# Feed-forward and conformer of a decoder step in passes over one token chunk, with vector operands kept in PSUM

## What is computed

```python
def swiglu(x, wg, wu, wd):
    return (jax.nn.silu(x @ wg) * (x @ wu)) @ wd

def conformer_conv(xn, buf, w_pw1, b_pw1, w_dw, b_dw, ln_g, ln_b, w_pw2, b_pw2):
    a, gate = jnp.split(xn @ w_pw1 + b_pw1, 2, axis=-1)
    h = a * jax.nn.sigmoid(gate)
    x_ext = jnp.concatenate([buf.astype(h.dtype), h], axis=1)
    buf_new = x_ext[:, -(CONV_W - 1):]
    h = causal_dwconv(x_ext, w_dw) + b_dw
    h = jax.nn.silu(layer_norm(h, ln_g, ln_b))
    return h @ w_pw2 + b_pw2, buf_new

# layer 0: x += mixer(rms_norm(x));      x += swiglu(rms_norm(x))
# layer 1: x += conformer(rms_norm(x));  x += swiglu(rms_norm(x));  y = rms_norm(x)
```

## Time and profile before

| | |
|---|---|
| median of 3 runs | 2816.01 us (2814.19 to 2819.28) |
| the profiled execution | 2820.21 us, of which the span 2818.4 us |
| PE, DVE, ACT, POOL busy | 98%, 50%, 31%, 24% of the span |
| chain that ended last | PE 62%, POOL 7%, DVE 2% |
| granted TensorE clock | 0.996 of full speed |

### The profile page before, as it was taken

How to read it: one execution, slowest core, us unless ns; L and a number is a source line. 1 busy time by engine, 2 the same in 40 slices (tenths; PEclk the granted TensorE clock), 3 DMA queues, 4 the chain that set the end, 5 groups by cost and what they waited for, 6 DMA issues and landing times.

```text
span 2818.4 us, 41854 instructions
## 1 busy us (share of the span) xinstructions
PE 2759.0 (98%) x15649; PEld 2419.5 (86%) x15649; DVE 1421.2 (50%) x2692; ACT 859.8 (31%) x1500; POOL 675.5 (24%) x333
## 2 busy tenths in 40 slices
PE   7999999999999999999999999999999999999998
PEld 5886666689866999999999986665699999999998
DVE  4227768889966532232232258997353222322325
ACT  2227739844423211111111034555221111111113
POOL 0210025511001322222222108991022222222220
PEclk9999999999999999999999999999999999999999
DMA  4220067634572211111111111110121111111101
GB/s 152 87 91 8 16 193 222 183 95 140 174 258 75 68 53 45 45 45 45 45 45 45 38 35 40 38 38 3 45 83 45 45 45 52 51 45 45 45 23 61
DMA packets 211508, 204.42 MB, mean 73 GB/s; under 512 B 10477, under 2 KB 165714, under 8 KB 211116
## 3 DMA queue, kind: packets, MB, share of 16 engines
q1 hardware_dynamic: 200014, 186.27, 21.7%
q0 software_dynamic: 2992, 12.26, 1.4%
q10 hardware_dynamic: 8390, 4.40, 0.6%
HBM read 187.59 MB, written 17.14 MB: 73 GB/s over the span
## 4 chain that ended last, share of the span: by engine, by line
PE 62%; POOL 7%; DVE 2%; DMA 1%; ACT 1%; issue 1%; SPq 0%; POOLq 0%; DVEq 0%; ACTq 0%
PE bank L2717 17%; PE bank L2718 17%; PE bank L2719 17%; POOL big L2994 6%; PE bank L364 3%; PE bank L2399 3%; PE bank L3047 1%; DMA res_b<-park 1%; PE bank L316 1%; POOL big L3000 1%; DVE tmp L303 1%; DVE res_b L2864 0%; DVE big L330 0%; DVE res_a L330 0%; ACT tmp L289 0%
## 5 line engine op out<-in xcount | busy, mean ns | idle before, releaser
L2717 PE MATMUL bank<-xh,wh 128*128 128x344 f32 x2112 | 675.3, 320 | 0.0
L2719 PE MATMUL bank<-xh,wl 128*128 128x344 f32 x2112 | 673.9, 319 | 0.0
L2718 PE MATMUL bank<-xl,wh 128*128 128x344 f32 x2112 | 673.5, 319 | 0.0
L2838 POOL TENSOR_TENSOR wl<-wring,wh 128x1024 fp32r<-128x1024 f32 x128 | 318.0, 2508 | 1111.1 <-ACT wh L2768 1111.0
L2856 DVE TENSOR_TENSOR tmp<-bank,tmp 128x344 f32<-128x344 f32 x132 | 68.1, 516 | 779.5 <-PE bank L2719 773.4
L2717 PEld LDWEIGHTS bank<-xh,wh 128*128 128x128 f32 x2112 | 397.4, 188 | 0.4
L2719 PEld LDWEIGHTS bank<-xh,wl 128*128 128x128 f32 x2112 | 396.7, 188 | 0.0
L2718 PEld LDWEIGHTS bank<-xl,wh 128*128 128x128 f32 x2112 | 396.0, 188 | 0.4
L2864 DVE TENSOR_TENSOR res_b<-res_b,bank 128x344 f32<-128x344 f32 x528 | 268.3, 512 | 199.7 <-PE bank L2719 199.5
L2717 PE MATMUL bank<-hh,wh 128*128 128x344 f32 x1056 | 339.2, 321 | 0.0
L2718 PE MATMUL bank<-hl,wh 128*128 128x344 f32 x1056 | 337.9, 320 | 0.0
(11 more groups left out here) (436 smaller groups left out, 3712.6 us busy)
## 6 DMA issues: line engine op xcount, KB each, us to landing
big<-in_cache_attn_k SPq DMA_DIRECT2D x128, 256.0 KB, 3.0
big<-in_cache_attn_v SPq DMA_DIRECT2D x128, 256.0 KB, 2.9
wring<-in_ffn_w_down SPq DMA_DIRECT2D x44, 512.0 KB, 3.3
wring<-in_ffn_w_gate SPq DMA_DIRECT2D x42, 512.0 KB, 3.8
wring<-in_ffn_w_up SPq DMA_DIRECT2D x42, 512.0 KB, 3.9
wring<-in_conv_w_pw SPq DMA_DIRECT2D x24, 512.0 KB, 4.0
wring<-in_w_in SPq DMA_DIRECT2D x20, 512.0 KB, 4.0
park<-res_a SPq DMA_DIRECT2D x1, 4128.0 KB, 11.2
```

The lines of the kernel that those rows point to most:

```text
L2717: pe.matmul(bank_out, h, mh, start=(n == 0), stop=False)
L2718: pe.matmul(bank_out, h, ml, start=False, stop=False)
L2719: mm = pe.matmul(bank_out, l, mh, start=False, stop=(n == len(terms) - 1))
L2838: pool.tensor_tensor(wl[u][:, :], raw, wh[u][:, :].bitcast(F32), ALU.subtract).then_inc(w_cut, 1)
```

## The change

The two feed-forwards and the conformer become one sequence (`late_pe`, `late_act`, `late_dve`, `late_pool`, `late_sp`) of six passes; pass p does all 11 rounds of a layer for one chunk. Passes 0 to 2 are layer 0 on chunks 0 to 2, passes 3 to 5 layer 1.

- Between the passes stand the pointwise products of the conformer for one chunk: pw1 of chunk 0 behind pass 1; pw2 of chunk 0 and pw1 of chunk 1 behind pass 2; pw2 of 1 and pw1 of 2 behind pass 3; pw2 of chunk 2 inside pass 4. Both now use three matmuls of cut operands, as the feed-forward does.
- The taps of chunk c are all on DVE, put between its other work in passes 2, 3 and 4 (`conv`): in a full round nine ahead of the first hidden product, one after each addition to x, nine ahead of the second. Two channel tiles are accumulated in turn in banks 4 and 5. `step.lagged` waits only for the instruction before the last one. PE and ACT have no taps; POOL sums the channel tiles for the mean (`mean_sum`).
- A round has six weight units as before but serves one chunk: 144 matmuls. The units are loaded and cut anew in each pass.
- A round runs up (tile 0), down of the round before, up (tile 1). Jobs turn through banks 0 to 3.
- The gated product stays in the PSUM bank of the up job; DVE cuts it from there. Roots go from ACT into a PSUM bank, and means are read from PSUM.
- Some low parts of x are made by POOL (`low`), some by DVE. Output blocks 0 to 4 are turned and stored during pass 5.

The core of the diff:

```diff
-            def up(i, t, c, u, first=False):
-                halves_in = (lambda v: pe.wait_ge(x_cut, f.x0 + 2 * c + v + 1)) if first and t == u == 0 else None
-                if c == 0:
-                    pe.wait_ge(w_cut, i * 6 + (f.units0 + 2 * t + u + 1))
-                j, s = 6 * t + 2 * c + u, 2 * t + u
-                g.wait_bank(pe, i, j)
...
-            def conv(n, part):
-
-                q1 = CW - pool_taps(n)
-                cut = [q1 * r // 3 for r in range(4)]
-                for q in range(cut[part], cut[part + 1]):
-                    src, w = glu[:, n, q:q + T].rearrange("p (v t) -> p v t", v=2), vec[:, n, V_WDW + q:V_WDW + q + 1]
-                    if q == 0:
-                        step(dve.tensor_scalar(acc(n), src, w, None, ALU.mult))
-                    else:
-                        step(dve.scalar_tensor_tensor(acc(n), src, w, acc(n), ALU.mult, ALU.add))
...
+        def job_bank(J):
+            return bank[:, (J - FIRST_JOB) % 4, 0:CH]
+
+        def norm_bank(nn, c):
+            return bank[:, 6 + nq(nn, c) % 2, 0:CH]
...
+        def root(act, nn, c, eps=1e-6):
+            q = nq(nn, c)
+            act.wait_ge(n_mm, q + 1)
+            act.activation(rstd[:, c, :], norm_bank(nn, c), ACT.Ln, scale=1.0 / D, bias=eps).then_inc(n_log, 1)
+            act.wait_ge(n_log, q + 1)
+            act.activation(norm_bank(nn, c), rstd[:, c, :], ACT.Exp, scale=-0.5).then_inc(n_rstd, 1)
+
+        def apply(dve, nn, c, src, dst, wv, ks=range(KD)):
+            dve.wait_ge(n_rstd, nq(nn, c) + 1)
+            for k in ks:
+                dve.scalar_tensor_tensor(dst[:, k, :], src[:, k, :], vcol(wv, k), norm_bank(nn, c), ALU.mult, ALU.mult).then_inc(n_out, 1)
...
+            def load(s, src, i=0):
+                sp.wait_ge(w_cut, lin(i, 6, ATT_UNITS + s - WQ + 1))
+                load_columns(s, raw_w[s % WQ], src)
...
+            def down(p, i, o=2):
+                wait_reads_before(pe, p, i, 0, 1)
+                hid = (hid_first[1 - odd(p, i)], hid_second)
+                wait_unit(pe, p, i, o + 1)
+                b = [(uoff(p, i) + o + k) % 6 for k in range(2)]
+                for n in range(KD):
+                    wait_job_bank(pe, p, i, o + n)
+                    cut_products(pe, job_bank(off(p, i) + o + n), [(wh[b[k]][:, n * P:(n + 1) * P], wl[b[k]][:, n * P:(n + 1) * P],
+                                 hid[k][0][:, :], hid[k][1][:, :]) for k in range(2)])
+
+            def body(p, i):
+                up(p, i, 0)
+                down(p, i)
+                up(p, i, 1)
...
+            def pw1(c):
+                for x in range(2 * KD):
+                    s, J = PW1_UNIT[c] + x, PW1_JOB[c] + x
+                    pe.wait_ge(w_cut, ATT_UNITS + s + 1)
+                    pe.wait_ge(free[J % 2], J // 2 + 2)
+                    columns_job(pe, J, s, PW1_SLOT, halves_cut(pe, 1, c) if x == 0 else None)
+                    if c and x == 5:
+                        sum_mm(pe, 4, c - 1)
...
+            for i in range(3):
+                body(2, i)
+            sum_mm(pe, 2, 1)
+            body(2, 3)
+            with pe.Fori(2, 4) as j:
+                body(2, (j, 0))
+                body(2, (j, 1))
+            up(2, 8, 0)
+            down(2, 8)
+            mean(0)
+            up(2, 8, 1)
+            up(2, 9, 0)
+            sum_mm(pe, 3, 0)
+            down(2, 9)
+            up(2, 9, 1)
+            body(2, 10)
+            pw2(0)
+            pw1(1)
...
+            def first_half(p, i):
+                silu(p, i, 0, 0)
+                cut(p, i, 0)
+                wait_job(act, p, i, 1)
+                cut(p, i, 1)
+
+            def downs_cut(p, i):
+                wait_job(act, p, i, 9)
+                cut(p, i, 2)
+                cut(p, i, 3)
+
+            def second_half(p, i):
+                silu(p, i, 1, 10)
+                cut(p, i, 4)
+                wait_job(act, p, i, 11)
+                cut(p, i, 5)
...
+            def unit(s, j=0, raw=None):
+                pool.wait_ge(wh_done, lin(j, 6, ATT_UNITS + s + 1))
+                pool.tensor_tensor(wl[s % 6][:, :], raw_w[s % WQ] if raw is None else raw, wh[s % 6][:, :].bitcast(F32), ALU.subtract).then_inc(w_cut, 1)
...
+            def hidden(p, i, t, o):
+                wait_job(dve, p, i, o + 1)
+                wait_job_read(dve, p, i, o)
+                d = job_bank(off(p, i) + o + 1)
+                hh, hl = hid_second if t else hid_first[odd(p, i)]
+                step(dve.tensor_tensor(d, d, gates_tmp[:, t, :], ALU.mult))
+                step(dve.tensor_copy(hh[:, :], d))
+                dve.tensor_tensor(hl[:, :], d, hh[:, :].bitcast(F32), ALU.subtract).then_inc(free[1], 1)
+
+            def add(p, i, n, o=2):
+                c = (p if not isinstance(i, int) or i else p - 1) % 3
+                J = off(p, i) + o + n
+                wait_job(dve, p, i, o + n)
+                d = x[:, n, chunk(c)]
+                dve.tensor_tensor(d, d, job_bank(J), ALU.add).then_inc(free[J % 2], 1)
+
+            def begin(p, i, taps=0):
+                conv(taps)
+                hidden(p, i, 0, 0)
+
+            def middle(p, i, taps=0):
+                for n in range(KD):
+                    add(p, i, n)
+                    conv(taps)
+
+            def end(p, i, taps=0):
+                conv(taps)
+                hidden(p, i, 1, 10)
...
+                    s = acc[v][:, 0:w]
...
+                        step.lagged(dve.tensor_scalar(s, src, col, vcol(V_BDW, k), ALU.mult, ALU.add))
...
+                        step.lagged(dve.scalar_tensor_tensor(s if q < CW - 1 else d, src, col, s, ALU.mult, ALU.add))
...
+            def conv_norm(p, c, i):
+                conv_rest(c)
+                begin(p, i)
+                middle(p, i)
+                centre(c)
+                end(p, i)
+                sums(dve, 3, c)
+                begin(p, i + 1)
+                middle(p, i + 1)
+                apply(dve, 3, c, conv_columns(c), conv_columns(c), V_LG)
+                end(p, i + 1)
+                low(dve, 2, c, CONV_SLOT[c])
+                body(p, i + 2)
...
+                for i in (4, 5, 6, 7):
+                    body(p, i, 9, 1, 9)
+                conv_norm(p, c, 8)
+                pw2(c)
+                pw1(c + 1)
...
+            begin(4, 10)
+            apply(dve, 4, 2, x[:, :, chunk(2)], x_scaled[:, :, chunk(SLOT[5])], V_FFN1, range(HK))
             for n in range(KD):
...
+                add(4, 10, n)
+                if n == 1:
+                    apply(dve, 4, 2, x[:, :, chunk(2)], x_scaled[:, :, chunk(SLOT[5])], V_FFN1, range(HK, KD))
+                if n == 3:
+                    low(dve, 4, 2, SLOT[5], (0,))
+                if n == 5:
+                    low(dve, 4, 2, SLOT[5], (1,))
+            end(4, 10)
```

More of the change, by code:

```diff
@@ L3292, in conf_dve @@
[L3292 to L3296 removed]
+                dve.wait_ge(hist_used, 1)
+            hidden(0, 0, 0, 8)
+            end(0, 0)
+            body(0, 1)
+            begin(0, 2)
+            middle(0, 2)
+            apply(dve, 1, 2, x[:, :, chunk(2)], x_scaled[:, :, chunk(2)], V_FFN0)
+            end(0, 2)
+            begin(0, 3)
@@ new lines, in late_dve @@
+            middle(0, 3)
+            stream_low(dve, f0, 2)
+            end(0, 3)
+            body(0, 4)
+            with dve.Fori(2, 4) as j:
+                step.enter(j - 2, 8)
+                body(0, (j, 1))
+                body(0, (j, 2))
+            step.leave(2)
+            begin(0, 9)
+            middle(0, 9)
+            history()
+            end(0, 9)
+            body(0, 10)
+            body(1, 0)
+            begin(1, 1)
+            middle(1, 1)
+            sums(dve, 2, 0)
@@ new lines, in late_dve @@
+            end(1, 1)
+            body(1, 2)
+            begin(1, 3)
+            middle(1, 3)
+            apply(dve, 2, 0, x[:, :, chunk(0)], x_scaled[:, :, chunk(PW1_SLOT)], V_MIX1)
+            end(1, 3)
+            body(1, 4)
+            with dve.Fori(2, 5) as j:
+                step.enter(j - 2, 8)
+                body(1, (j, 1))
+                body(1, (j, 2))
+            step.leave(3)
+            pw1(0)
+            for p, c in ((2, 0), (3, 1)):
+                body(p, 0, 9, 1, 8)
+                begin(p, 1, 9)
+                middle(p, 1, 1)
+                sums(dve, 2, c + 1)
+                end(p, 1, 4)
+                body(p, 2, 9, 1, 8)
+                begin(p, 3, 9)
+                middle(p, 3, 1)
+                apply(dve, 2, c + 1, x[:, :, chunk(c + 1)], x_scaled[:, :, chunk(PW1_SLOT)], V_MIX1)
+                end(p, 3)
+                for i in (4, 5, 6, 7):
+                    body(p, i, 9, 1, 9)
+                conv_norm(p, c, 8)
+                pw2(c)
+                pw1(c + 1)
@@ new lines, in late_dve @@
+            apply(dve, 5, 1, x[:, :, chunk(1)], xn[:, :, chunk(2)], V_FIN)
+            end(5, 3)
+            with dve.Fori(2, 5) as j:
+                step.enter(j - 2, 8)
```

(10 more changed lines are left out.)

1308 lines of the change are left out of this document (679 added, 629 removed).

## The result

| | before | changed |
|---|---|---|
| median of the runs, us | 2817.65 (2814.19 to 2819.66, 4 runs) | 2726.36 (2723.96 to 2728.6, 4 runs) |
| ratio, 95% interval | 1 | 0.9677 (0.966 to 0.9694) |
| profiled execution / its span, us | 2820.2 / 2818.4 | 2728.6 / 2726.8 |

A forecast was written before the change was run, and what follows sets the result against it. PE, busy 98% of the span, was taken as the bound: its work and pace behind 910 us count. -113.6 + 11.4 - 4.5 + 0.6 + 12 = -94.1 us; 2816.0 - 94.1 = 2722 us, range 2710 to 2765.

The forecast's parts named there:

- PE's conformer, -113.6 us: Conformer: pw1 and pw2 as 1,728 cut matmuls, 271.3 us on PE, against 384.9 us for the whole conformer before.
- rival 4: Behind 910 us, PE's pace does not hold: at 0.160 us a matmul, 34 us more, 2756; chance 0.19 together with Rival 1.
- Feed-forward in another order, no change: Both feed-forwards: 9,504 matmuls on PE before and after, only in another order, 1,492 us both times.
- small work +11.4: PE between jobs: norm sums, means and turns take 22.9 us in place of 11.5.
- The end, -4.5: Kernel end: five output blocks are already out, only chunk 2 is left; 4.5 us less.
- The start, +0.6: Start of the late part: unit 2's cut by POOL ready about 918.2, where PE asks at 917.7; 0.6 us more.
- The others keep up: Rounds behind 910 us: DVE 19.6 us, POOL 14.6, ACT 7.2 fit under PE's 22.6, so the 744 taps are hidden.
- Rival 1: DVE is full: 0.62 us a tap makes its round 23.5 us, total 2752; chance 0.19 together with rival 4.
- No blocking of VectorE and GpSimd: DVE's work in the rounds has a PSUM operand, so the taps should not wait for POOL.
- Rival 2: POOL's six cuts a round block DVE: round 34 us, 232 us more over 20 rounds, total 2954; chance 0.03.
- rival 3: Weights come too late: 4.1 us a unit at 8.6 us to land, 168 us more, total 2890; chance 0.04.
- The waits, 12 us: PE's waits: 2 us on each of three chunks' layer norms, 1.5 for late taps, 4 in pass 4's last round; 3 to 30.

The follow-up runs named there:

- the scalings: Changed kernel with the roots of the norms kept in SBUF, so that the scalings read two SBUF tensors: 2765.18 us, late stream 36.2 us longer.

## Why the prediction was right, point by point

- **What bounds it, and PE's conformer, -113.6 us.** Right. The late stream keeps 0.157 us a matmul through all passes, with loads at three times the rate beside it (rival 4 is out). Adding 576 matmuls costs 92.7 us, undoing the cut 63.9.
- **Feed-forward in another order, no change; small work +11.4.** Right. 11,158 distances between cut matmuls in the stream average 0.157 us. Counted as the forecast does (from the first start of a small matmul to the second cut one behind it, less one pace), the small work of the stream is 23.0 us instead of 22.9: norm sums 14.4, means 1.7, turns 6.9.
- **The end, -4.5.** 4.6.
- **The start, +0.6.** The size is met by other waits than the one named. The wait for unit 2's low part shows as 0.31 us of a weight load at 916.13; PE waits 0.40 us for a silu and 0.52 for a hidden product, which the forecast did not see.
- **The others keep up.** Right, and by its numbers: the round 19.2 us instead of 19.6, the tap 0.57 and 0.48 apart instead of 0.59 and 0.50. POOL 1,345 us busy (1,340 forecast), ACT 1,143 (1,150), DVE 1,604 (1,660: my forecast was 56 us too high, on no step that the sum used). Rival 1's 0.62 a tap is refuted; its round of 23.5 us would lie between the two runs with more taps (22.4 us for 9.8 us, 25.3 for 58.9).
- **No blocking of VectorE and GpSimd.** Right for PSUM operands. Rival 2's mechanism was shown with the sums in SBUF: 255 us, of which 175 are the waits that its 232 stood for.
- **The weights in time (rival 3).** Right that three buffers suffice. The step that names the waiter was wrong: a late load is felt through ACT's list, not at PE's wait for the cut.
- **The waits, 12 us.** The sum is right by luck, the parts are not. The places that the forecast names cost 5.5 us: the three layer norms, put at 2 us each, 0.43 each, a sum that comes just too late; chunk 2's late taps 0.82 instead of 1.5; the last round of pass 4 3.4 instead of 4. Not seen were 5.9 us: the norm sum of chunk 1 in pass 5, 2.87 us (it stands one job too early in PE's list), 1.72 us in front of the last down job, which has nothing ahead of it that could hide its hidden product, and two more short waits for a hidden product at 1520.73 and 1865.81 (0.68, 0.65). With the 0.9 of the start that makes PE's 12.4 us of idle time.
- **What the sum left out.** The terms give 1,799.0 us for the stretch where 1,803.6 were measured. The missing 4.6 us are in no wait: they are the single distances between starts of 0.2 to 0.4 us, to which the sum gave no term. That the span came out nearer, 91.6 us against 94.1, is luck too: 2.0 us of the fall lie ahead of 908 us, where nothing was changed.

So the mechanism held: PE's count of matmuls at its pace sets the time, and the rest is hidden. Of the small terms one was met only in sum, and one was missing.

## What to carry to other kernels

When one engine is busy 98% of the time, price every instruction of its list by the pace of two starts in the trace, and count; the forecast of a 91 us change was then within 5. For the others compute a round's sum against that engine's round, but also look at single places: a delay longer than the idle time ahead of the next product that PE needs is paid, as the scalings showed, and it can travel by a third engine's list. Where VectorE works beside a GpSimd stream, give each of its instructions a PSUM operand: the place of the taps' two accumulators was worth 255 us. And where a change makes PE wait, add the clock that the waits cost, next section.
